# Channel-major residual, norms by a ones-matmul, keys transposed by DMA, in an eight-core hybrid trunk on Trainium2

## The reference

```python
def rmsnorm(x, g):
    return x * lax.rsqrt(jnp.mean(x * x, axis=-1, keepdims=True) + EPS) * g

def pool_mixer(h, w_in, w_grp, scale, w_out):          # 4 groups of 512 channels, windows 2, 4, 8, 16
    u, z = jnp.split(h @ w_in, 2, axis=-1)             # 2048 each
    pooled = trailing_mean(u, w) - u                   # per group; the mean leaves out the padding
    y = jnp.einsum('blgc,gcd->blgd', pooled, w_grp)
    return (y * scale * jax.nn.silu(z)) @ w_out

def gla_mixer(h, w_in, w_gate2, b_gate, head_norm, w_out):    # 4 heads, dk 256, dv 512
    q, k, v, z, glr = split(h @ w_in)
    log_a = jax.nn.log_sigmoid(glr @ w_gate2 + b_gate) / 16
    # per chunk: cum = cumsum(log_a); qe = q exp(cum) / 16; ke = k exp(-cum); kd = k exp(g_tot - cum)
    #   o = tril(qe ke^T) v + qe S;   S = exp(g_tot) S + kd^T v
    o = o * lax.rsqrt(jnp.mean(o * o, axis=-1, keepdims=True) + EPS) * head_norm     # per head
    return (o * jax.nn.silu(z)) @ w_out

# h = h + mixer(rmsnorm(h, norm_i)) for 4 layers; out = rmsnorm(h, final_norm)[:, 16:]
```

## Time and profile before

| | us |
|---|---|
| median of 3 runs (2202.59 to 2203.53) | 2203.27 |
| profiled execution: span of the slowest core (core 7), the time of that execution | 2214.9 |
| spans of the other cores | 2195.1 to 2214.9 |
| TensorE busy | 1978.5 (89%) |
| VectorE, ScalarE, GpSimd busy | 1327.1, 1365.1, 428.5 |

### The profile page before, as it was taken

The page is one execution under the profiler, slowest core; times in us unless marked ns, Lnnn a source line. Parts: engine busy times, 40 slices in busy tenths (PEclk is TensorE's granted clock), DMA queues, the critical chain, the costliest instruction groups (busy, mean ns, idle before and its releaser), DMA issues.

```text
span 2214.9 us, 46775 instructions; the slowest of 8 cores (2195.1 to 2214.9 us)
## 1 busy us (share of the span) xinstructions
PE 1978.5 (89%) x16712; PEld 1406.1 (63%) x16712; DVE 1327.1 (60%) x2151; ACT 1365.1 (62%) x2903; POOL 428.5 (19%) x468
## 2 busy tenths in 40 slices
PE   0289999987999999996775999999989999999997
PEld 0267777765766777664443666777656676777764
DVE  1245555775776666664443445557857766666787
ACT  2455555576676677675544545555766666676776
POOL 1012345673000000000000113447730000000000
PEclk9899999999999999998876789999999999999998
DMA  9313132303013040020201131423030040400011
GB/s 187 96 30 58 18 61 39 59 10 61 1 23 57 2 78 2 2 49 1 39 3 27 29 47 21 68 39 58 1 67 2 9 70 2 78 2 1 21 68 67
DMA packets 16691, 86.07 MB, mean 39 GB/s; under 512 B 2624, under 2 KB 3536, under 8 KB 9296
## 3 DMA queue, kind: packets, MB, share of 16 engines
q0 software_dynamic: 10560, 63.53, 17.0%
q1 hardware_dynamic: 5904, 19.57, 2.6%
HBM read 138.22 MB, written 8.39 MB: 66 GB/s over the span
## 4 chain that ended last, share of the span: by engine, by line
PE 79%; DVE 6%; issue 5%; ACT 4%; POOL 3%; DMA 2%; SPq 0%; DVEq 0%; ACTq 0%; POOLq 0%
PE ps L401 77%; DVE hnb L432 2%; DMA h<-x 2%; PE ps L409 2%; POOL SB L437 2%; ACT hnb L426 1%; DVE h L432 1%; POOL SA L437 1%; DVE Y L437 1%; ACT gs L426 1%; ACT rstd L426 1%; ACT hnT L426 1%; DVE S L432 0%; DVE SB L432 0%; DVE sz L432 0%
## 5 line engine op out<-in xcount | busy, mean ns | idle before, releaser
L401 PE MATMUL ps<-hnT,W 128*128 128x256 bf16 (+1 forms) x9216 | 988.0, 265 | 12.9 <-ACT vb L426 5.9
L401 PEld LDWEIGHTS ps<-hnT,W 128*128 128x128 bf16 x9216 | 834.8, 99 | 148.5 <-issue 26.8
L401 PE MATMUL ps<-W,Y 128*128 128x512 bf16 x1024 | 249.8, 386 | 15.8 <-DVE Y L437 9.3
L401 PE MATMUL ps<-W,hnT 128*128 128x512 bf16 x1088 | 261.6, 385 | 0.6 <-DVE sz L432 0.6
L437 DVE TENSOR_TENSOR h<-h,ps 128x512 f32<-128x512 f32 x256 | 175.0, 684 | 129.7 <-PE ps L401 127.6
L401 PE MATMUL ps<-W,yT 128*128 128x512 bf16 x1024 | 250.0, 387 | 0.3 <-DVE S L432 0.3
L432 DVE SCALAR_TENSOR_TENSOR h<-ps,rs,h 128x512 f32<-128x512 f32 x256 | 191.0, 746 | 98.5 <-ACT rs L426 56.8
L442 POOL COPY el<-Eq 128x2 f32<-128x2 f32 x136 | 26.4, 194 | 988.3 <-ACT Eq L426 760.6
L426 ACT ACTIVATE Sb<-S,el 128x512 bf16<-128x512 f32 x256 | 183.3, 716 | 47.0 <-DVE S L432 29.9
L432 DVE SCALAR_TENSOR_TENSOR S<-S,el,ps 128x512 f32<-128x512 f32 x240 | 176.9, 737 | 58.7 <-PE ps L401 57.4
L432 DVE SCALAR_TENSOR_TENSOR sz<-ps,vec,gs 128x256 bf16<-128x256 f32 (+2 forms) x288 | 129.9, 451 | 118.3 <-ACT rs L426 60.6
(11 more groups left out here) (87 smaller groups left out, 2456.0 us busy)
## 6 DMA issues: line engine op xcount, KB each, us to landing
W<-wpack POOLq DMA_DIRECT2D x56, 1024.0 KB, 9.8
h<-x SPq DMA_DIRECT2D x16, 512.0 KB, 44.8
out<-h SPq DMA_DIRECT2D x16, 512.0 KB, 2.7
W<-wpack POOLq DMA_DIRECT2D x8, 512.0 KB, 6.3
gbc<-gains SPq DMA_DIRECT2D x5, 512.0 KB, 3.9
Wglr<-wglrp POOLq DMA_DIRECT2D x2, 132.0 KB, 26.0
wg<-wg2p POOLq DMA_DIRECT2D x8, 33.0 KB, 2.2
hm<-metaT SPq DMA_DIRECT2D x1, 64.0 KB, 12.6
```

The lines of the kernel that those rows point to most:

```text
L401: ins = e.matmul(o_, lhsT=l_, rhs=r_, start=st, stop=sp_)
```

## The change

The residual `h` becomes channel-major, [128, 8, 2064] float32 with the meta tokens in it, loaded in the 9 blocks (9 DMAs on SP; blocks 2 and on are issued only after weight tiles W3, W1 and W2 of the first unit) and stored in 9. The norm of a block is `norm1` (two squares over 4 x n on ScalarE, the second into the bytes of hnT that it will overwrite, three adds on GpSimd, a bfloat16 high part and the remainder) and, three slots later, `norm2` (two matmuls with a ones matrix, Ln and Exp over n columns, eight VectorE operations that write hnT). No stream transposes and no gain broadcast are left. The output product has the weights stationary, streams y with up to 256 columns, two groups a bank, four banks' worth a block. In GLA the head norm is a ones-matmul over the block of o squared, summed by two GpSimd adds a tile; its rs multiplies y on GpSimd (`scale`) ahead of the output product. kd comes from ke by two DMA transposes a block on SP. S is two tensors, Sb two pairs; one of a pair is written by ScalarE and one by GpSimd. A block's scan is one instruction over 512, with a zero at each segment's start (`seg`), and its masks one product. The low-rank gate is four 32-column groups, summed by repeating the second weight four times.

Work is issued by slots: `defer(k, fn)` runs fn k slots later; residual products, norms, scales and fold pieces go so. Pool groups are taken in the order of windows 4, 16, 8, 2. The costs of the kernel's own model are changed, and `refine` plans a second time: every engine but TensorE takes what a TensorE operation needs soonest. The scratch for GpSimd's DMA descriptors is 4096 bytes.

```diff
+GROUPS = (1, 3, 2, 0)
+LAG = {2: 2, 4: 2, 8: 4, 16: 4}
...
+    def refine(self):
+        need = [float("inf")] * len(self.ops)
+        for o in reversed(self.ops):
+            for u in o.users:
+                if u.eng == "pe":
+                    t = u.start
+                else:
+                    t = need[u.i] - u.dur - u.tail
+                need[o.i] = min(need[o.i], t - self.SEM)
+        for o in self.ops:
+            if o.eng != "pe":
+                o.prio = (need[o.i] - o.dur, o.i) if need[o.i] < float("inf") else (self.span, o.i)
...
+    def norm1(bi):
...
+        hf = hnT[:, :, c0:c0 + n].bitcast(F32).rearrange("p (k a) m -> p k a m", a=2)
+        qa = sqA[:, :, 0:n].rearrange("p k (a m) -> p k a m", a=2)
+        act([hb[bi]], [b_sqA], sqA[:, :, 0:n], h[:, 0:4, c0:c0 + n], AF.Square)
+        act([hb[bi]], hts, hf, h[:, 4:8, c0:c0 + n].rearrange("p k (a m) -> p k a m", a=2), AF.Square)
+        tt("pool", [b_sqA] + hts, [b_sqA], qa, qa, hf, ALU.add)
+        tt("pool", [b_sqA], [b_sqA], sqA[:, 0:2, 0:n], sqA[:, 0:2, 0:n], sqA[:, 2:4, 0:n], ALU.add)
+        tt("pool", [b_sqA], [b_sqA], sqA[:, 0, 0:n], sqA[:, 0, 0:n], sqA[:, 1, 0:n], ALU.add)
+        copy("pool", [b_sqA], [b_sqh], sqh[:, 0:n], sqA[:, 0, 0:n])
+        tt("pool", [b_sqA, b_sqh], [b_sql], sql[:, 0:n], sqA[:, 0, 0:n], sqh[:, 0:n], ALU.subtract)
+
+    def norm2(li, bi):
...
+        mm([b_sqh, b_sql, b_ones], [bank[sbk]], [(PS[sbk][:, 0:n], ones[:], sqh[:, 0:n], True, False),
+                                                 (PS[sbk][:, 0:n], ones[:], sql[:, 0:n], False, True)])
+        r = rb[k_][:, 0:n]
+        act([bank[sbk], b_eps], [b_rb[k_]], r, PS[sbk][:, 0:n], AF.Ln, scale=1.0 / D, bias=epsc[:, 0:1], psum=True)
+        act([b_rb[k_]], [b_rb[k_]], r, r, AF.Exp, scale=-0.5)
...
+                stt([hb[bi], b_rb[k_], b_gT], hts, hnT[:, kc, c0:c0 + n], h[:, kc, c0:c0 + n], gT[:, li * 8 + kc:li * 8 + kc + 1], r,
+                    ALU.mult, ALU.mult)
...
+    def resid(bi, Wo, wb, y, yb, lo):
...
+        for g in range(4):
+            b = out_bank()
+            po = PS[b][:, 0:2 * w].rearrange("p (f m) -> p f m", f=2)
+            mm([yb, wb], [bank[b]],
+               [(po[:, f, :], Wo[:, kc, (2 * g + f) * 128:(2 * g + f + 1) * 128], y[:, kc, lo:n], kc == 0, kc == 3)
+                for f in range(2) for kc in range(4)])
+            hh = h[:, 2 * g:2 * g + 2, c0 + lo:c0 + n]
+            tt("dve", [bank[b], hb[bi]], [hb[bi]], hh, hh, po, ALU.add)
...
+                        if n == 256:
+                            P.dma("sp", "kd%d" % par, lambda q, dc=dc: q.dma_start_transpose(out=kd[:, dc, :, :], in_=ke[:, dc, :]),
+                                  [b_ke], [b_kd], 65536, 1000.0)
...
+        def scale(k_):
...
+            mm([A["os"], b_ones], [bank[3]], [(PS[3][:, lo:n], ones[:], os[:, lo:n], True, True)])
+            act([bank[3], b_eps], [A["rs"]], rs[:, lo:n], PS[3][:, lo:n], AF.Ln, scale=1.0 / 512, bias=epsc[:, 0:1], psum=True)
+            act([A["rs"]], [A["rs"]], rs[:, lo:n], rs[:, lo:n], AF.Exp, scale=-0.5)
+            tt("pool", [A["yt"], A["rs"]], [b_sz], sz[:, :, lo:n], yt[:, :, lo:n],
+               rs[:, lo:n].unsqueeze(1).to_broadcast([128, 4, n - lo]), ALU.mult)
...
+            z(k_)
+            slot()
+            att(k_)
+            v(k_)
+            kv(k_, 0)
+            slot()
+            core(k_, 0)
+            qk(k_ + 1, 0)
+            if nt > 1:
+                kv(k_, 1)
+            qk(k_ + 1, 1)
+            slot()
+            if nt > 1:
+                core(k_, 1)
+            gates(k_ + 2)
+            defer(1, lambda k_=k_: scale(k_))
...
+            defer(2, finish)
```

More of the change, by code:

```diff
@@ L509, in fold @@
         wgv = wg.rearrange("p (fc n) -> p fc n", fc=4)
-        for mt in range(8):
+        for mt in (2 * part, 2 * part + 1):
             b = proj_bank()
@@ L556, in load_gain, with fold_later @@
-    def load_gain(li):
-        dma("sp", "gbc", gbc[:], gains[li:li + 1, :].partition_broadcast(128), [], [b_gbc], 524288)
-    def norm_block(li, bi, b):
-        for t_ in BLOCKS[bi][0]:
-            if t_ == 0:
-                norm_meta(li, b)
-            else:
-                norm_tile(t_, b)
-    def glr_block(bi, b):
+    def fold_later(ui):
+        if ui < len(units) and units[ui][0] % 2 == 0:
+            for part in range(4):
+                defer(part + 1, lambda part=part: fold(ui, part))
@@ L567, in glr_block @@
+    def glr_block(bi):
         tiles, c0, n = BLOCKS[bi]
+        b = statb[0]
         mm([hnTb[t_] for t_ in tiles] + [b_wglr], [bank[b]],
[L569 to L575 removed]
@@ L599, in pool_layer @@
     def pool_layer(li, ui0):
         j = li // 2
-        nproj[0] = 4
-        order = range(4)
-        for gi in order:
+        projs[0] = (0, 1, 2, 3)
+        outs[0] = (4, 5, 6)
+        statb[0] = 7
+        for gi in range(4):
             ui = ui0 + gi
-            u = units[ui][1]
+            u = GROUPS[gi]
             w = WINS[u]
@@ new lines, in pool_block @@
+                slot()
+                if li == 0 and gi == 0:
+                    if bi == 0:
+                        for part in range(4):
+                            fold(0, part)
+                    if bi + 1 < NB:
+                        norm2(0, bi + 1)
+                    if bi + 2 < NB:
+                        norm1(bi + 2)
+                if bi == 0:
+                    P.op("pool", lambda e, U=U: e.memset(U[:, :, 0:16], 0.0), [], [A[Un]], 200.0)
+                else:
+                    pn = BLOCKS[bi - 1][2]
+                    copy("pool", [A[Uo]], [A[Un]], U[:, :, 0:16], Up[:, :, pn:pn + 16])
@@ L898, in build @@
         (pool_layer if li % 2 == 0 else gla_layer)(li, 4 * li)
+    for _ in range(40):
+        slot()
+    P.schedule()
+    P.refine()
     P.schedule()
@@ L970 @@
     res = run_bass_kernel_spmd(nc, in_maps, core_ids=list(range(_cores)))
-    return np.stack([res.results[b]["out"] for b in range(_cores)], axis=0)
+    return np.stack([tokens_of(res.results[b]["out"]) for b in range(_cores)], axis=0)
```

716 lines of the change are left out of this document (352 added, 364 removed).

## The result

The changed kernel takes **2090.54 us** (median of 4 runs, 2086.91 to 2139.23) where the kernel before takes 2203.40 beside it: ratio 0.9486, 95% interval 0.9470 to 0.9502, or 5.1% faster. The forecast was 1960 us, range 1885 to 2075. The direction was right, and the gain (113 us) was under half of the one foretold (243). In some runs the cores of one die show a lower granted clock and take longer (here the 2139.23, and one of 2377.45 of the kernel before); ratios leave such runs out, and the spans given with the experiments are those of cores 0 to 3, which were free of it in every profiled run.

The account below looks back on a forecast made before the run. TensorE was taken as the bound, with norms stalling it at the start and in the first GLA layer's last head. 1837 + 28 + 5 + 21 + 28 + 20 + 15 + 5 + 11 = 1970, less 11.6: 1960 us, range 1885 to 2075.

Parts of the forecast that it names:

- The port: VectorE operations with two SBUF inputs run in turn with GpSimd's, not beside them, so the two engines' times add up.
- Floor: TensorE's time where nothing holds it: 1837 us after the change, 51 less than before.
- Start: Before the first z: it comes at 28 us, when its loads have landed, plus 5 us for a low clock.
- First unit: Window-4 pool unit of layer 0: GpSimd and VectorE together take 15.3 us a block; 21 us lost.
- window-2 units: Last pool unit of a pool layer: 114 us with gaps against 100, so 14 us lost, twice.
- last heads: Last GLA heads, where norms are made: 18.1 us a block against 16.9, 10 us lost a head, twice.
- rival B: Every VectorE norm operation waits out a GpSimd operation, so VectorE carries both: 2070 us; chance 0.12.
- Rival A: The port hardly binds, norm operations find gaps, and the unit, head and hand-over losses go: 1885 us; chance 0.2.
- Rival E: Norms leave TensorE but still hold it, their ones-matmul queued behind GpSimd's chain: 2180 us; chance 0.03.
- Low clock: TensorE's clock is low at first, costing 5 us; otherwise it was taken as 1.00.
- Rival D, keys by DMA: Key transposes by DMA outlast their 13.7 us of cover; at 20 us a pair, 2363 us; chance 0.07.
- Rival C, the chain into resid: Scaling sz by rs before the output product stalls TensorE by 1.5 us in 72 blocks: 2068 us; chance 0.1.

Follow-up runs that it names:

- experiment 9, first kernel: Changed kernel with one edit: ScalarE writes the eight squares as bf16 and eight ones-matmuls add them; 1981 to 1987 us, ratio 0.9061.
- experiment 2: Changed kernel with x's second half block behind scales and vector table: 2082 to 2085 us; with second unit's weights also held until the first fold: 2091 to 2095.
- experiment 1: Changed kernel with the norm's rs written to PSUM, so its eight last VectorE operations have one SBUF input: 2044 to 2051 us.
- the new start: Changed kernel, rs in PSUM, scales ahead of x's second half block, later weights and x blocks held until the first fold: 2026 to 2036 us, ratio 0.9268.
- the best version: Changed kernel with rs in PSUM, the new start, keys on TensorE and squares added by eight ones-matmuls: 1979 to 1983 us, ratio 0.9019.

## Why the prediction was wrong

**The step that failed** is the norm in "The change part by part": "Norm adds over 1024, 512 and 256 elements, a cast and a subtraction: 1.9 + 1.15 + 3 x 0.6 = 4.9 us", and with it the use made of that number in "The port". I counted GpSimd's norm work as load that is added to VectorE's, block by block; outside the tail the sum never has it as a chain, and never as something that holds up other work in GpSimd's queue. It is a chain: last square, five operations in an in-order queue that also holds the pool's adds, ones-matmul, Ln, Exp, eight operations on VectorE. The five take 5.7 us by their means and 8.3 (median) with what stands between them, 11.8 pass until the ones-matmul, and the eight last operations take 10.0, against 4.9 and 3.8. Taking the five off GpSimd (experiment 9, first kernel) takes 126 us of the loss and brings it to 128 us. The forecast's was 133, so this one step is as large as the miss. That the rest comes so near 133 is in part luck: with the edit the start still costs 48 us where 33 were forecast, and the first and the two last pool units 16 where 49 were. Which property of the five costs most, their length or their place in GpSimd's queue, is not shown; see "What stays open".

Point by point:

- *Floor*: 1837 forecast, 1836 by the same count in the trace, 1830 with the gate's matmuls as measured. Right. The removal of the transposes from TensorE and the end of the slow head of the earlier trace rows were the gain, as said; but that head takes 167 us at a clock of 0.94 where 145 to 155 at 1.00 was my sign for the main step, so the sign was not met.
- *Start* (28 + 5): 50. I counted the loads that the first z needs, and not gT, nor its place behind x on SP's queue. But the runs of experiment 2 show that this is not 22 us to be had: weights and x share the DMA engines, 97% busy in the first 50 us, and only the whole new order gave 17, or 2 once the norm was cured.
- *First unit* (21), *window-2 units* (2 x 14), *last heads* (2 x 10): 41, 25 + 23, 42 and (up to 2070) 35. With the norm off GpSimd they are 9, 4 + 3, 13, and 20 for the last head and the tail together. The port was half right: such operations do wait out GpSimd's (experiment 1, 35 us), but most of those they met were the norm's own adds: with these gone the operation fell from 895 to 630 ns, of the 478 that it takes alone. Of the two operations of rows 8 that I rested the port on, the cast has only one SBUF input and is not of the norm's kind; experiment 1 is what shows the port. GpSimd's other work was dearer too: a state copy takes 1.66 us where I had 1.15. My reason against rival B, "the eight stand back to back, with hardly room for GpSimd between them", was wrong: the planner orders by need and sets them singly among h adds and window operations.
- *Rival B* (2070) was nearest in time, and its mechanism is in the trace; but rs in PSUM, which ends it, brings 35 us and not 110. Rival A (1885) wants 69 us from norm operations that find gaps: with the norm off GpSimd the unit terms without the last head are some 29 us (131 in the changed kernel), but the start stays at 48.
- *Rival E* (2180, 0.03) named the ones-matmul that stands behind GpSimd's chain, nearest to the step that failed. As a direct wait it is small: TensorE waits 20.2 us for sql in all, 13.4 of it at the start.
- *Low clock* (5): by busy time x (1 - clock) 35 us, all behind idle gaps. This was a consequence: I carried over the 1.00 of the stretches of the earlier trace rows with TensorE over 85% busy, and the unit of 50 to 200, 83% busy, had 0.90.
- *Rival D, keys by DMA*: no. They land in 2.3 us (median) and at most 13.9, the edge of the 13.7 of cover. Yet they were not free: twice the keys on TensorE, with 14 us more floor, came out 7 to 10 faster, and once level. Where those 14 to 24 us lie was not settled. In 700 to 800, a stretch with no norm, the loss was 5, 8 and 6 us with the DMA and 1 to 2 without it, in the changed kernel, with the new start and in the best version.
- *Rival C, the chain into resid*: small. TensorE waits 12.4 us for sz in all, 5.6 of it for one product in the tail.
- *Middle heads*: TensorE is idle for 7.6 us in 508 to 950, under the 10 that was a sign of being wrong.
- *Tail* (11): 15 behind 2070, and part of the 35 before it: GpSimd's product, output matmuls, GpSimd's norm, eight operations, twice, with nothing beside them. With the squares added on TensorE the last ones-matmul waits 2.3 us instead of 5.8 (single edit).
- *I am wrong if ... the first unit takes over 140*: it took 150 from 50 to 200 us.

What stays open. The parts taken one by one are 35 (rs in PSUM) and 50 (adds left out); the single edit takes 126 us of loss. Some of the rest is the clock, 35 us before and 6 after, and in the first 200 us the loss falls from 92 to 58 with no change to the loads. That the parts overlap is shown: rs in PSUM and the new start are worth 35 and 17 ahead of the edit and 2 behind it. What in the chain costs, its length or the GpSimd time it takes in the very units where the pool's adds are due, is not told apart. The waits speak for both: of the 95 us of idle time that went, some 35 were waits for the norm's own results and some 34 waits for Y, h and sz, which only share the queues with it. The one buffer sqA is not the cause: ScalarE's squares waited 2.8 us in all for it. The chain's length is hard to price from the traces: the interval from the squares to the ones-matmul holds slack (in the best version, with nothing on GpSimd, it is still 8.6 us, since the order places the ones-matmul slots later; in the single edit 5.1), and one GpSimd operation did as well as none, in a kernel that can mix up two norms' sums.
